# A hybrid recurrent decoder layer on one core: the gated-linear heads without a loop, and two weight splits per head moved

## What is computed

```python
def _gla_branch(q, k, v, g_lo, zb, state, gk_w2, gk_b, norm_w, front):
    g = jax.nn.log_sigmoid(g_lo.astype(f32) @ gk_w2 + gk_b) / GATE_TAU
    q = q.astype(f32) * (B_HK ** -0.5)
    def step(S, inp):                      # a chunk of 64 tokens
        qc, kc, vc, gc = inp
        b = jnp.cumsum(gc, axis=2)
        o = jnp.einsum('nhtk,nhkv->nhtv', qc * jnp.exp(b), S)
        diff = b[:, :, :, None, :] - b[:, :, None, :, :]
        dec = jnp.exp(jnp.where(mask, diff, -jnp.inf))
        att = jnp.einsum('nhtk,nhsk,nhtsk->nhts', qc, kc, dec)
        o = o + jnp.einsum('nhts,nhsv->nhtv', att, vc)
        b_last = b[:, :, -1:, :]
        S = S * jnp.exp(b_last)[:, :, 0, :, None] + jnp.einsum('nhsk,nhsv->nhkv', kc * jnp.exp(b_last - b), vc)
        return S, o
    ...
    o = o * lax.rsqrt(jnp.mean(o * o, axis=-1, keepdims=True) + NORM_EPS) * norm_w.astype(f32)
    o = o.reshape(n, t, B_VDIM) * jax.nn.silu(zb.astype(f32))
```

## Time and profile before

| | us |
|---|---|
| median of 3 runs | 2988.94 (2987.89 to 2996.24) |
| the profiled execution | 2991.96 |
| its span, first to last instruction | 2990.4 |
| mean granted TensorE clock in it | 0.987 |

### The profile page before, as it was taken

How to read it: one execution, slowest core, us unless ns; L and a number is a source line. 1 busy time by engine, 2 the same in 40 slices (tenths; PEclk the granted TensorE clock), 3 DMA queues, 4 the chain that set the end, 5 groups by cost and what they waited for, 6 DMA issues and landing times. The chain is left out here.

```text
span 2990.4 us, 78906 instructions
## 1 busy us (share of the span) xinstructions
PE 2876.0 (96%) x33575; PEld 2701.6 (90%) x33575; DVE 1737.1 (58%) x2594; ACT 1072.0 (36%) x1818; POOL 405.4 (14%) x812
## 2 busy tenths in 40 slices
PE   7999999999997999999999999999999999997997
PEld 6998998998986899899999999999999999996997
DVE  5455544636635576576675675675675665765323
ACT  4332432424322243243243343243343343343332
POOL 5001001001004022021021021021121120121000
PEclk9999999999998999999999999999999999998998
DMA  5224324324323222132132132222222222222522
GB/s 162 77 71 142 108 57 155 109 57 155 108 85 122 60 75 74 45 88 73 46 84 73 51 81 68 58 74 67 67 74 66 67 74 62 71 73 96 161 85 92
DMA packets 368508, 255.29 MB, mean 85 GB/s; under 512 B 19380, under 2 KB 347568, under 8 KB 366256
## 3 DMA queue, kind: packets, MB, share of 16 engines
q1 hardware_dynamic: 342560, 184.18, 22.6%
q0 software_dynamic: 25600, 66.02, 7.0%
HBM read 212.69 MB, written 37.45 MB: 84 GB/s over the span
## 5 line engine op out<-in xcount | busy, mean ns | idle before, releaser
L204 PE MATMUL psum<-act_hi,w_hi 128*128 128x280 f32 (+1 forms) x4672 | 1423.7, 305 | 14.5 <-DVE w_lo L190 8.9
L206 PE MATMUL psum<-act_hi,w_lo 128*128 128x280 f32 (+1 forms) x4672 | 1363.4, 292 | 0.7 <-issue 0.7
L205 PE MATMUL psum<-act_lo,w_hi 128*128 128x280 f32 (+1 forms) x4672 | 1362.3, 292 | 0.3 <-issue 0.3
L204 PEld LDWEIGHTS psum<-act_hi,w_hi 128*128 128x128 f32 (+1 forms) x4672 | 880.7, 189 | 66.8 <-issue 36.4
L205 PEld LDWEIGHTS psum<-act_lo,w_hi 128*128 128x128 f32 (+1 forms) x4672 | 879.9, 188 | 5.1 <-issue 1.6
L206 PEld LDWEIGHTS psum<-act_hi,w_lo 128*128 128x128 f32 (+1 forms) x4672 | 879.6, 188 | 0.0
L190 DVE TENSOR_TENSOR w_lo<-raw,w_hi 128x1024 fp32r<-128x1024 f32 (+1 forms) x324 | 396.2, 1223 | 286.3 <-ACT w_hi L182 276.7
L182 ACT CAST w_hi<-raw 128x1024 fp32r<-128x1024 f32 (+1 forms) x324 | 339.5, 1048 | 32.4 <-DMA raw<-in_w_out_dram 15.0
L1701 POOL DMA_DIRECT2D out_s_rwkv_dram<-arena x128 | 77.5, 613 | 1320.6 <-ACT arena L1853 1160.8
L2173 PE MATMUL psum<-arena 64*64 64x64 f32 x9984 | 206.5, 223 | 21.0 <-issue 14.8
L2173 PEld LDWEIGHTS psum<-arena 64*64 64x64 f32 x9984 | 182.3, 134 | 46.5 <-issue 44.3
(11 more groups left out here) (342 smaller groups left out, 3510.1 us busy)
## 6 DMA issues: line engine op xcount, KB each, us to landing
raw<-in_w_in_dram SPq DMA_DIRECT2D x288, 512.0 KB, 4.3
arena<-in_state_gla_dram POOLq DMA_DIRECT2D x32, 512.0 KB, 5.1
out_s_gla_dram<-arena POOLq DMA_DIRECT2D x32, 512.0 KB, 3.3
raw<-in_w_out_dram SPq DMA_DIRECT2D x32, 512.0 KB, 4.6
ob_dram<-arena POOLq DMA_DIRECT2D x16, 280.0 KB, 3.2
arena<-ob_dram POOLq DMA_DIRECT2D x16, 280.0 KB, 4.8
m_dram<-arena POOLq DMA_DIRECT2D x16, 280.0 KB, 2.6
act_lo<-m_dram SPq DMA_DIRECT2D x1, 4200.0 KB, 16.7
```

Source lines behind the costliest of these rows:

```text
L204: pe.matmul(out, hi, act_hi[:, k, cols], start=(k == 0), stop=False)
L205: pe.matmul(out, hi, act_lo[:, k, cols], start=False, stop=False)
L206: mm = pe.matmul(out, lo, act_hi[:, k, cols], start=False, stop=(k == KT - 1))
```

## The change

Three things are changed. The hardware loop over heads 0 to 2 becomes a Python loop on all five engines, so that all four heads are written out, and the registers with which the loop computed its semaphore values and addresses are gone. `split_hi` and `split_lo` of tile 6 move behind `level_exps(2)` and `take(1)`, `factors(2)`. `gate_of(0, 1)` with `split_hi` of tile 10, and `gate(0, 1)` with `split_lo` of tile 10, move behind the exponentials and the products of the decayed keys.

```diff
                 for t in range(5):
                     load(0, t)
-                with sp.Fori(0, LAST_HEAD) as i:
+                for i in range(LAST_HEAD):
                     for t in range(5, 17):
                         load(i, t)
...
-                with pool.Fori(0, LAST_HEAD) as i:
-                    head_of(i)
-                head_of(LAST_HEAD, last=True)
+                for i in range(BH):
+                    head_of(i, last=i == LAST_HEAD)
...
                     evacuate(i, 4, 1)
+                    level_exps(2)
                     pc.split_hi(act, i, mine, 6)
-                    level_exps(2)
                     evacuate(i, 5, 0)
...
                     decays(0)
                     decays(1)
-                    gate_of(0, 1)
-                    pc.split_hi(act, i, mine, 10)
                     for n in range(2):
                         act.wait_ge(kd_diff.sem, kd_diff.at(i, n + 1))
                         activation(qk[n], qk[n], ACT.Exp, scale=1.0 / 16).then_inc(kd_exp.sem, 1)
                         act.wait_ge(kd_exp.sem, kd_exp.next(i))
+                    gate_of(0, 1)
+                    pc.split_hi(act, i, mine, 10)
                     kd_to_sbuf(0)
...
                     diff(2)
-                    pc.split_lo(dve, i, mine, 6)
                     take(1)
                     factors(2)
+                    pc.split_lo(dve, i, mine, 6)
                     diff(3)
...
                     rows(3)
-                    gate(0, 1)
-                    pc.split_lo(dve, i, mine, 10)
                     for n in range(2):
                         dve.wait_ge(kd_exp.sem, kd_exp.at(i, n + 1))
                         tt(qk[n], qk[n], k_g[n], MUL).then_inc(kd_ready.sem, 1)
                         dve.wait_ge(kd_ready.sem, kd_ready.next(i))
+                    gate(0, 1)
+                    pc.split_lo(dve, i, mine, 10)
                     dve.wait_ge(ends_ready.sem, ends_ready.at(i, 2))
```

More of the change, by code:

```diff
@@ L855, in head_of @@
                         mine.close()
-                with act.Fori(0, LAST_HEAD) as i:
-                    head_of(i)
-                head_of(LAST_HEAD, last=True)
+                for i in range(BH):
+                    head_of(i, last=i == LAST_HEAD)
             @block.vector
@@ L1153, in head_of @@
                         mine.close()
-                with dve.Fori(0, LAST_HEAD) as i:
-                    head_of(i)
-                head_of(LAST_HEAD, last=True)
+                for i in range(BH):
+                    head_of(i, last=i == LAST_HEAD)
             @block.tensor
@@ L1399, in head_of @@
                         pass
-                with pe.Fori(0, LAST_HEAD) as i:
-                    head_of(i)
-                head_of(LAST_HEAD, last=True)
+                for i in range(BH):
+                    head_of(i, last=i == LAST_HEAD)
         with nc.Block() as block:
```

## The result

| | before | changed |
|---|---|---|
| median, us | 2988.94 (5 runs, 2984.86 to 2996.24) | 2973.29 (5 runs, 2972.90 to 2975.51) |
| ratio, 95% interval | | 0.9945 [0.9934, 0.9955] |
| the profiled execution, us | 2991.96 | 2974.18 |

The changed kernel is faster by 0.55%, 15.7 us by the medians; 2976.0 was forecast, a gain of 12.9. In the profiled executions the difference is 17.8 us.

What follows compares the result with a forecast made beforehand. PE, busy 96% of the span, bounds the kernel, so time is won only where it waits in the heads: 3.5 + 5.8 + 3.6 = 12.9 us off the median 2988.94 gives 2976.0 us; range 2971 to 2981, with rivals 2970.5 to 2982.5.

Steps and rivals of the forecast that it cites:

- Part 1: Level 2's grams: with tile 6's split behind level 2, PE's whole wait goes in four heads, 3.5 us.
- The step that adds 0.16 us to each idle row: PE's waits: the timeline draws matmuls overlapping, so each such wait loses its idle time plus 0.16 us.
- Part 2: Transposition of decayed keys: with the gate and tile 10's split behind them, PE's wait goes in four heads, 5.8 us.
- The covers named for tiles 6, 10 and 11 and for bank 1: Work made later by the moves still arrives before PE needs it; covers of 8, 5 and 4 us were among those named.
- Part 3: Ends of heads: writing out the loop removes PE's idle at its jumps back, 3.6 us, bounds 0 and 3.8.
- The control: Branch falling through into head 3: same ACT work, no PE wait, so the jump back and not line 672 is the cause.
- term (b): RWKV turns: 19 unexplained PE waits, 14.8 us, always on line 2173, dealt anew with the same sum, 3 us either way.
- Term (a): Heads: the granted-clock drop seen in head 1 cost 1.7 us and may come in none or two heads, 1.7 us either way.
- A: Ends of heads: PE waited for ACT's line 672, so the loop is worth nothing; 9.3 us gain, 2979.6 us; chance 0.08.
- B: Heads: removed waits come back at the next level or product, the order worth nothing; 3.6 us gain, 2985.3 us; chance 0.08.
- C: RWKV turns: late instructions hit twice as many dense stretches of line 2173, adding 14.8 us, 2990.8 us; chance 0.04.
- D: Between heads: a jump remains, so the change doesn't do what it says; no chance of its own.

Runs made afterwards that it cites:

- undo_tile6: The changed kernel with tile 6's split put back ahead of level 2 on ACT and DVE; one execution, 2979.68 us.
- pe_written_out: The kernel before with PE's loop alone written out, other loops and both splits as before; ratio 0.9992, 2989.45 us against 2990.38.
- order_only: The kernel before with both splits moved and all loops kept; ratio 0.9949, 2977.74 us against 2990.38.

## Why the prediction was right

**What bounds the kernel.** PE's waits in the heads, three places, held. With them gone PE's busy time is the same to 1.1 us (2876.0 and 2874.9), and the time fell.

**Part 1, 3.5 us forecast.** 3.4 us by undoing it. The spare time was put at 3.1 us and is 3.2. The step that adds 0.16 us to each idle row was needed: the waits sum to 2.5 us in undo_tile6, 3.1 with that step, and undoing gave 3.4. A part of the loop's gain was here too: with the loops written out the wait was 2.4 and not 2.9 us to begin with.

**Part 2, 5.8 us forecast.** 5.8 us. Spare time forecast 2.9 us, measured 3.1. The covers named for tiles 6, 10 and 11 and for bank 1 held: no new wait.

**Part 3, 3.6 us forecast.** 3.8 us: 2.13 and 1.65 at the two jumps, by the trace with PE and DVE written out. The control, no wait at the branch of 83 ns, had pointed the right way. But the prediction gave the whole to PE's jump and set DVE's jump aside as "off the path". That step was wrong as stated: DVE's jump of 3.06 us lay behind PE's and would have taken 2.2 of the 3.8 us, as it did when PE was written out alone. The change writes both out, so the sum was right although the reason was half of it; that part of it was luck. That a taken branch to code outside the fetched window stalls (the Trainium skill, Runtime: NRT & Kernel Launch, section Instruction fetch mechanics) agrees with both engines' jumps, 3.3 to 4.0 us of PE's sequencer and 3.06 us of DVE, and on PE with the packets that begin during each of them.

**Sum.** 12.9 us forecast, 13.3 us in the heads. Line 1376 was to keep its 0.9 us and has 1.2.

**What the sum lacked.** The gain was 15.7 us by the medians, and the interval of the ratio, 13.5 to 19.7 us, begins just above the 12.9 that were forecast; by the traces it was 18.0. Ahead of the first k-step lies 1.0 us of this, and 3.7 us behind the heads, where the instructions are the same. The waits for issue of all lines behind the heads fell from 15.7 to 13.2 us, 2.5 of the 3.7. Two of those before, 0.7 and 0.3 us, stood on lines 206 and 205, so the waits were not "always on line 2173". For the waits alone the 3 us either way of term (b) held, 14.8 and 13.2 us on that line. For the whole stretch they are too narrow: over the thirteen other traces it lies between 6.0 us below and 2.6 us above that of the kernel before, eleven of them below. The one trace from which the sum started was likely on the slow side there; that trace was not taken again, so this stays open. Term (a) came to nothing, since one head has the clock drop in both traces; a drop costs 1.6 us where 1.7 was reckoned.

**Rivals.** A is wrong by pe_written_out, B by order_only and the two undone moves, C did not come: 13.2 us of waits for issue after 14.8. D had no place.

## To carry to other kernels

Look at what DVE and ACT idle for just ahead of the work that the bound engine waits for; if it is work that nobody needs yet, put that behind, and check each thing that is then later against the moment when it is needed. A hardware loop with a long body costs each engine its own jump, here 3 to 4 us on PE and on DVE, and on ACT 0.5 us with a table load of 1.28 us behind it; the jumps hide each other, so taking one away shows little (0.6 us in the heads, 1.1 for the other four engines) and taking away both shows 3.8. An idle row in the trace understates the loss where the timeline draws instructions overlapping: measure start to start.

## What the hardware showed that was not expected

**The waits at block ends.** In streams of 64 by 64 products PE runs out of instructions where its list goes on to the next 256, up to 1.7 us each, at about one block end in eleven. That it waits for the block to arrive can be read from q8. Pair each block end in the turns and behind them with its packet of 16 KB, in order: in all fourteen traces none was passed sooner than 2.2 us after the packet had begun; the 276 waits over 0.15 us ended 2.2 to 3.0 us after it, and where PE did not wait the distance was 6.5 to 6.8 us in the middle. In the streams a block lasts some 4.8 us, in the heads 14 to 20 us by the packets' starts, and no wait for issue appears there. The same code at the same place of the list gave sums of 10.6 to 14.8 us in eight traces; what delays one packet and not another was not tried. The same section of the Trainium skill calls going on into the next block mostly hidden: the traces agree for the heads and for ten block ends of eleven in the turns, and the rest cost 7.8 to 14.8 us in all.

**The clock drop has a place.** The drop of the earlier trace rows came again in most traces, always some 3.4 us at 1.2 in place of 2.4 GHz, and always 34 to 37 us behind the sum of squares of a head, just behind the small products of 32 and 48 columns and those with 16 rows (lines 1381, 1383 and 1206). In the changed kernel it is in head 0, and the same work of head 1 has none (columns as in the earlier trace rows, the granted clock third from the end):

```profile
296.00:306.00 10.00, 10.00 (x58) 8.65 (x58) 0.00 (x0) 0.68 (x2) 0.00 (x0) 0.83 0.33 86
506.00:516.00 10.00, 10.00 (x75) 9.37 (x74) 1.50 (x2) 2.92 (x4) 0.00 (x0) 1.00 0.01 2
```

A head that has it is 1.6 us longer than the same head without it. In fourteen traces, with three such heads each, it came fourteen times; in three of the four with the half split moved it did not come at all, which may be chance. What decides it was not tried.

**Semaphore increments on PE.** In a row they start 0.15 us apart though each is drawn 51 ns long: 64 take 9.8 us between the heads and the turns, 128 take 19.6 us at the head of the list (starts from 0.9 to 20.3 us). Where PE waits anyway only what goes beyond the wait is lost, 2.4 us behind the heads.
